# The long-convolution filter moved into the steps of expert layer 0

## The chip, the core and the metric

The kernel runs on one core of one Trainium2 chip. The metric is the device time of one execution in microseconds. Before the change it is 1826.23 us, the median of three runs (1824.58 to 1829.15).

## What is computed

Two blocks of a diffusion backbone over 256 tokens of width 1024, plus 256 context tokens in the first block, all in float32. Block 0 mixes tokens with a bidirectional RWKV, block 1 with an order-2 Hyena operator; after each comes a mixture of experts with 32 experts, top-2. Cut to what matters here:

```python
def _hyena_filters(L, f_w1, f_b1, f_freq, f_wi, f_bi, f_w3):       # needs weights only, no tokens
    hdn = jnp.sin(f_freq * (z @ f_w1 + f_b1))                      # 33 -> 64
    for n in range(2):
        hdn = jnp.sin(f_freq * (hdn @ f_wi[n] + f_bi[n]))          # 64 -> 64
    h = (hdn @ f_w3).reshape(L, 2, 2, D) * jnp.exp(-t * deltas)    # 64 -> 2 orders x 2 signs x 1024
    kern = jnp.concatenate([h[:, :, 0], 0, flip(h[1:, :, 1])])
    return kern / jnp.sum(jnp.abs(kern), 0)
def _fft_conv(u, kern, skip):                                      # twice in _hyena_seq
    return irfft(rfft(u) * rfft(kern))[:L] + u * skip
def expert_block(args):                                            # for each of 32 experts
    return (silu(xb @ w_gate[e]) * (xb @ w_up[e])) @ w_down[e]     # 1024x512, 1024x512, 512x1024
```

## The kernel before

The program is a row of blocks with a barrier between them: RWKV, `expert_layer` for layer 0, `hyena_layer` (two blocks, `hyena_inputs` and `hyena_convolutions`), `expert_layer` for layer 1, and the final norm. SBUF is one arena in which every stage lays out its own tiles by column.

**Expert layer.** All 32 experts' weights are streamed through SBUF once in each layer: 96 units of 2 MB (128 partitions with one row of 16 KB each), in the order gate, up, down of each step. Ten steps: steps 0 to 3 are wide (two experts, six units), steps 4 to 9 narrow (four experts, twelve units, numbers 24 to 95). The units go round a ring of `SLOTS_OF` = 10 slots of the arena. `expert_units` writes the order by hand: for each unit its slot and the unit that held the slot before. SP, in program order, waits (`unit_done`) until that earlier unit's product has ended and issues the load (line 1770; the last step's down units are cut into quarters, line 1768). Semaphore `block_in` tells TensorE of the landing. The first `FIRST_UNITS` = 6 units are issued in the stage before. A small batch of loads that the next stage needs (`gate_b`, `hyena.load_small`, the 1154 KB `hy_const`) stands ahead of unit 88 in the same queue.

TensorE's order in step i: gate product (line 1935, bank G), up product (line 1935, bank U), gather of step i+1's tokens (line 1922, banks X0 and X1), turning the hidden rows (lines 1963 and 1965), scatter of step i-1 (line 1983), down product (line 1945, into X0 and X1). A product of a narrow step needs all four units of its kind and frees all four at its end. ScalarE applies the Silu to G, turns tokens and copies the down result out of X0 and X1 (`copy_rows`, lines 2073 and 2074, semaphore `y_ready`). VectorE multiplies gate by up (`hidden_rows`, line 2149) and, in steps 1 to 3, works through twelve possible extra expert slots (`take_extras`, then `count_extras`, line 2295).

**`hyena_inputs`.** 24 input products `in_block` (line 2579), each of 16 instructions of 256 columns, with the filter's pieces placed between them by hand (`taps_after`, `spectrum_after`): three sine layers (`argument`, `sine`), the taps times a window (`taps`, `windowed`, lines 2712 to 2716), forward transforms (`spectrum`, line 2551; `combine`), sums of magnitudes (`absolute`, `magnitudes`, `turn_magnitudes`). **`hyena_convolutions`** transforms the values, multiplies by `khat` and transforms back, then the output product. SP starts layer 1's expert units here: two at the start, then four after `y_done` reaches 8; units 6 to 9 follow at the start of layer 1.

## Time and profile before

| | us |
|---|---|
| median of three runs | 1826.23 |
| the profiled execution | 1815.37 |
| its span in the trace | 1813.2 |
| layer 0 stream, first issue to last chunk used | 619 to 1106 |
| `hyena_inputs` | 1119 to 1247 |
| `hyena_convolutions` | 1247 to 1335 |
| layer 1 | 1335 to 1803 |

All rows come from the one profiled execution; times in them are microseconds from the start of its span. The page divides the span into 40 slices. A line of the timeline merges consecutive instructions of a kind; the bracket gives the engine's idle time before it and what ended it. "PE" is TensorE, "DVE" VectorE, "ACT" ScalarE, "SPq" and "ACTq" the queues on which SP and ScalarE issue transfers. For a transfer the timeline's duration is the time in which the issuing queue was held, not the transfer's. TensorE's granted clock is given as a share of its full 2.4 GHz.

### The profile page before, as it was taken

How to read it: one execution, taken by the hardware profiler on the slowest of the kernel's cores; microseconds unless marked ns; L12 is line 12 of the kernel's file. 1: busy time of each engine (PE TensorE's matmuls, PEld its weight loads, DVE VectorE, ACT ScalarE, POOL GpSimd, SP SyncE). 2: the span in 40 equal slices, each digit the busy share in tenths (PEclk: the TensorE clock that was granted, in tenths of full speed). 3: DMA queues.
4: the chain of work that ended last, by engine and by line, in shares of the span. 5: the costliest groups of instructions: out<-in, count | busy, mean ns of one | idle time of the engine just before them, and what ended most of it. 6: DMA issues, size and time to landing. Idle time of an engine off the chain costs nothing. (4 is left out here: it accounts for less than half of the span.)

```text
span 1813.2 us, 35471 instructions
## 1 busy us (share of the span) xinstructions
PE 1412.5 (78%) x14647; PEld 781.5 (43%) x14647; DVE 758.6 (42%) x1952; ACT 448.8 (25%) x857; POOL 57.9 (3%) x53
## 2 busy tenths in 40 slices
PE   5879999999986989966455737998899985557545
PEld 2446766676665443422122203776544341222111
DVE  5767787778764365400000001766757510000001
ACT  3244565456543031110000002213131110000001
POOL 0001100110010000000000001000000000000001
PEclk8989999999998999987787769999999997887788
DMA  9023334424445599999999997224279999999995
GB/s 333 1 63 100 105 115 133 125 89 130 118 138 191 183 427 427 426 427 427 428 428 428 427 384 274 93 93 185 77 322 393 425 428 427 427 427 428 427 426 224
DMA packets 108946, 504.55 MB, mean 278 GB/s; under 512 B 16224, under 2 KB 61040, under 8 KB 83952
## 3 DMA queue, kind: packets, MB, share of 16 engines
q1 hardware_dynamic: 107520, 501.93, 69.9%
q8 instruction: 118, 1.93, 0.4%
q10 hardware_dynamic: 1264, 0.33, 0.1%
q14 instruction: 44, 0.36, 0.1%
HBM read 501.13 MB, written 1.09 MB: 277 GB/s over the span
## 5 line engine op out<-in xcount | busy, mean ns | idle before, releaser
L1935 PE MATMUL banks<-arena 128*32 128x512 f32 (+1 forms) x2048 | 326.1, 689 | 241.7 <-DMA arena<-in_moe_w_gate 121.6
L1935 PEld LDWEIGHTS banks<-arena 128*32 128x32 f32 (+1 forms) x2048 | 97.7, 131 | 467.6 <-issue 464.0
L2149 DVE TENSOR_TENSOR arena<-banks,arena 128x512 f32<-128x512 f32 x20 | 13.8, 692 | 631.3 <-PE banks L1935 631.0
L1945 PE MATMUL banks<-arena 128*32 128x512 f32 (+1 forms) x1024 | 147.0, 615 | 32.0 <-DMA arena<-in_moe_w_down 29.9
L788 PE MATMUL banks<-arena 128*128 128x512 f32 (+1 forms) x384 | 158.7, 551 | 0.0
L2063 ACT ACTIVATE arena<-banks,arena 128x128 f32<-128x128 f32 x80 | 30.1, 457 | 303.2 <-PE banks L1922 303.2
L1945 PEld LDWEIGHTS banks<-arena 128*32 128x32 f32 (+1 forms) x1024 | 46.2, 119 | 129.6 <-issue 121.7
L788 PEld LDWEIGHTS banks<-arena 128*128 128x128 f32 x384 | 70.3, 196 | 52.5 <-issue 44.3
L2579 PE MATMUL banks<-arena 128*128 128x256 f32 x384 | 87.4, 386 | 0.0
L2579 PEld LDWEIGHTS banks<-arena 128*128 128x128 f32 x384 | 73.5, 193 | 16.7 <-issue 6.6
L1922 PEld LDWEIGHTS banks<-arena 128*128 128x128 f32 x640 | 73.0, 192 | 16.7 <-issue 14.9
L1922 PE MATMUL banks<-arena 128*128 128x128 f32 x640 | 76.8, 278 | 0.1
L2054 ACT ACTIVATE arena<-banks 128x512 f32<-128x512 f32 x20 | 11.9, 597 | 260.8 <-PE banks L1935 260.8
L1983 PE MATMUL banks<-arena 128*128 128x512 f32 x160 | 72.2, 594 | 2.4 <-ACT arena L2074 2.4
L2073 ACT ACTIVATE arena<-banks 128x512 f32<-128x512 f32 x20 | 11.9, 597 | 211.7 <-PE banks L1945 211.7
L253 PE MATMUL banks<-arena 128*32 128x96 f32 (+1 forms) x1536 | 46.5, 260 | 12.4 <-DMA arena<-in_ada_w 11.1
L2061 DVE TENSOR_SCALAR arena<-banks,arena 128x128 f32<-128x128 f32 x80 | 27.3, 403 | 53.5 <-PE banks L1922 53.5
L253 PEld LDWEIGHTS banks<-arena 128*32 128x32 f32 x1536 | 35.0, 110 | 21.5 <-issue 17.7
L1983 PEld LDWEIGHTS banks<-arena 128*128 128x128 f32 x160 | 28.8, 190 | 32.9 <-issue 28.7
L1214 ACT ACTIVATE arena<-x_res,const 128x256 f32<-128x256 f32 x64 | 42.2, 733 | 1.4 <-DVEq L1469 0.6
L2349 POOL TENSOR_TENSOR x_res<-x_res,arena 128x512 f32<-128x512 f32 x8 | 9.9, 1265 | 971.7 <-DVEq L2323 971.7
L2287 DVE TENSOR_TENSOR arena<-arena 128x128 f32<-128x128 f32 x120 | 35.1, 292 | 9.6 <-issue 0.7
(412 smaller groups left out, 2293.0 us busy)
## 6 DMA issues: line engine op xcount, KB each, us to landing
arena<-in_moe_w_gate SPq DMA_DIRECT2D x64, 2048.0 KB, 25.2
arena<-in_moe_w_up SPq DMA_DIRECT2D x64, 2048.0 KB, 27.0
arena<-in_moe_w_down SPq DMA_DIRECT2D x56, 2048.0 KB, 25.2
arena<-in_ada_w SPq DMA_DIRECT2D x128, 192.0 KB, 3.0
arena<-in_ada_w SPq DMA_DIRECT2D x64, 256.0 KB, 3.6
arena<-in_moe_w_down SPq DMA_DIRECT2D x32, 512.0 KB, 17.1
arena<-in_rw_wrkv SPq DMA_DIRECT2D x24, 512.0 KB, 5.2
arena<-in_hy_w_in SPq DMA_DIRECT2D x6, 2048.0 KB, 8.6
```

The source lines that it names most:

```text
L253: mm = pe.matmul(bank[g * 32:(g + 1) * 32, 0:n], self.cond[:, half * self.HALF + t], self.w[t][:, g * n:(g + 1) * n], start=(t == 0), stop ...
L788: mm = pe.matmul(s.psum[OPEN.bank(n, name)][:, 0:width], wkv[k][:, t], x[:, t], start=(t == 0), stop=(t == KT - 1))
L1214: act.activation(to, v, ACT.Identity, scale=flag(d))
L1922: mm = pe.matmul((X0, X1)[k // 4][:, k % 4 * P:(k % 4 + 1) * P], hx[:, t, k * P:(k + 1) * P], sel[:, t], start=(t == 0), stop=(t == TT - 1))
L1935: mm = pe.matmul(bank[j * rows:(j + 1) * rows, :], xT[:, t, j * rows:(j + 1) * rows], w[:, t], start=(t == 0), stop=(t == KT - 1), tile_po ...
L1945: mm = pe.matmul(bank[j * rows:(j + 1) * rows, :], hT[:, t, j * rows:(j + 1) * rows], w[:, k, half * 512:(half + 1) * 512], start=(t == 0) ...
L1983: pe.matmul(OUT[k][:, :], selwT[par][:, k // 2], y[:, k % 2 * 512:(k % 2 + 1) * 512], start=start, stop=stop).then_inc(scat_done, 1)
L2061: op = eng.tensor_scalar(xT[:, k], src, sc[:, k:k + 1], sh[:, k:k + 1], ALU.mult, ALU.add)
L2063: op = eng.activation(xT[:, k], src, ACT.Identity, bias=sh[:, k:k + 1], scale=sc[:, k:k + 1])
L2149: dve.tensor_tensor(h, U[:, :], h, ALU.mult).then_inc(h_ready, 1)
L2287: dve.tensor_tensor(prod, pick, src, ALU.mult)
L2579: mm = pe.matmul(s.psum[n % 2][:, 0:L], win_ring[k][:, t, q * P:(q + 1) * P], hT[:, t], start=(t == 0), stop=(t == KT - 1))
```

## The change

The filter leaves `hyena_inputs`. A new class `HyenaFilter` computes it in eleven pieces inside expert layer 0 (`FILTER_WORK`): two in each of steps 3 to 7, ahead of the gate product and ahead of the up product, and one in step 8. Pieces 0 to 2 are the sine layers. Pieces 3 to 10 each take a quarter of the 1024 channels of one order: taps, window, forward transform, sum and difference into `khat`, magnitudes, reciprocal. They run in banks X0 and X1, so TensorE waits in front of each for `y_ready`, and the gather waits for the pieces' reads.

The filter's small weights and half of `hy_const` are now issued by SP ahead of unit 18 (`load_constants`). The output weights of the filter and the decay rates come in four quarters, issued on ScalarE's queue (`load_quarter`): quarter 0 at the start of step 4, and quarter q+1 when ScalarE has done the second piece of quarter q, since one buffer serves all. Each quarter is two transfers of 64 partitions x 2 rows and two of 128 rows, rows of 1 KB.

The spectra, constants and scratch take over ring slots of layer 0: slots 8 and 9 leave the ring at unit 10, slot 7 at unit 24 and slot 3 at unit 84, so that ten slots become eight, seven and six. In layer 1 only slot 3 leaves, at unit 84 (before, slot 8 left at 79). With the new tables a unit's slot was held before it, in layer 0, by: unit 18 by 10; 29 by 22; 31 by 24; units 32 to 83 by the unit seven before; 90 by 84 and 94 by 88. `hyena_inputs` keeps the 24 input products. Layer 1's unit 0 is issued at its end, unit 1 after the second `imag_ready`, units 2 and 3 after `y_done` reaches 8, and from unit 4 on at the start of layer 1.

```diff
-FIRST_UNITS = 6
-TAIL_UNITS = 79
...
+LAST = 3
+RETIRED = ({WORK: 10, TAIL: 10, 7: 24, LAST: 84}, {LAST: 84})
+FIRST_UNITS = (6, 4)
...
-                if slot == TAIL and n >= TAIL_UNITS:
-                    slot = WORK
+                while n >= retired.get(slot, n + 1):
+                    slot = (slot + 1) % SLOTS_OF
...
-UNITS, LAST_IN = expert_units()
+UNITS, LAST_IN = zip(*(expert_units(r) for r in RETIRED))
+N_UNITS = len(UNITS[0])
...
-            for n in range(SLOTS_OF, len(UNITS)):
-                step = UNITS[n][0]
...
+            now, early, late = None, fil is not None, True
+            for n in range(SLOTS_OF, N_UNITS):
+                step, used = units[n][0], units[n][6]
                 if step >= FIXED // 2 and step != now:
                     now = step
                     first, count = (2 * step - FIXED, 2) if step < WIDE_STEPS else (HOT + 4 * (step - WIDE_STEPS), 4)
                     if step == FIXED // 2:
                         sp.wait_ge(moved_ready, 1)
                     of = [sp.value_load(moved_i[0:1, k:k + 1], min_val=0, max_val=EXPERTS - 1) for k in range(first, first + count)]
-                sp.wait_ge(unit_done, UNITS[n][6] + 1)
-                if UNITS[n][6] == LAST_IN[TAIL] + 1:
+                sp.wait_ge(unit_done, used + 1)
+                if early and used > last_in[TAIL] and used > last_in[WORK]:
+                    early = False
+                    fil.load_constants(sp, ins)
+                if late and used > last_in[LAST]:
+                    late = False
                     sp.dma_start(gate_b, experts.mod_row(mods, 5).partition_broadcast(P)).then_inc(gate_in, 16)
                     if hyena is not None:
                         hyena.load_small(sp, ins, mods)
                 experts.load_unit(sp, ins, n, fixed(step) if step < FIXED // 2 else of)
             if hyena is not None:
                 for b in range(hyena.SLOTS):
-                    sp.wait_ge(unit_done, LAST_IN[b] + 1)
+                    sp.wait_ge(unit_done, last_in[b] + 1)
                     hyena.load_ring(sp, ins, b)
...
+            if fil is not None and isinstance(i, int):
+                fil.banks_read(pe, i - 1)
...
                 tokens_ready(pe, i)
+                if fil is not None and (i, 0) in FILTER_WORK:
+                    pe.wait_ge(y_ready, i)
+                    fil.multiply(pe, FILTER_WORK.index((i, 0)))
                 hidden_product(pe, i, "gate", G)
+                if fil is not None and (i, 1) in FILTER_WORK:
+                    pe.wait_ge(y_ready, i)
+                    fil.multiply(pe, FILTER_WORK.index((i, 1)))
                 hidden_product(pe, i, "up", U)
                 if i + 1 < N_STEPS:
...
             for i in range(N_STEPS):
+                if fil is not None and i == EXTRA // 4 + 1:
+                    act.wait_ge(extra_ready, 1)
+                    fil.load_quarter(act, ins, 0)
+                if fil is not None and (i, 0) in FILTER_WORK:
+                    fil.activate(act, ins, FILTER_WORK.index((i, 0)))
                 silu_gate(act, i)
+                if fil is not None and (i, 1) in FILTER_WORK:
+                    fil.activate(act, ins, FILTER_WORK.index((i, 1)))
                 if i + 1 < N_STEPS:
                     turned_rows(act, range(4, KT), i + 1).then_inc(xT_act, 1)
...
+                for gap in range(2):
+                    if fil is not None and (i, gap) in FILTER_WORK:
+                        fil.combine(dve, FILTER_WORK.index((i, gap)))
                 hidden_rows(dve, i)
...
+    def load_constants(self, sp, ins):
+        hy = self.hy
+        for n, v in enumerate((ins["hy_f_freq"][0], ins["hy_f_b1"][0], ins["hy_f_bi"][0, 0], ins["hy_f_bi"][0, 1])):
+            sp.dma_start(hy.fv[0:FH, n:n + 1], v.unsqueeze(1)).then_inc(hy.w_in, 16)
+            if n in (0, 3):
+                sp.dma_start(hy.fv[FH:P, n:n + 1], v.unsqueeze(1)).then_inc(hy.w_in, 16)
+        sp.dma_start(hy.w1[0:EMB, :], ins["hy_f_w1"][0]).then_inc(hy.w_in, 16)
+        sp.dma_start(hy.wi[0:FH], ins["hy_f_wi"][0].rearrange("n i o -> i n o")).then_inc(hy.w_in, 16)
+        sp.dma_start(hy.hc, ins["hy_const"][:, 0:HY_EARLY]).then_inc(hy.hc_in, 16)
+
+    def load_quarter(self, act, ins, q):
+        c = slice(q * 256, (q + 1) * 256)
+        for od in range(2):
+            rows = ins["hy_f_w3"][0, :, od * 2 * D:(od + 1) * 2 * D].rearrange("r (a n) -> r a n", a=2)
+            act.dma_start(self.hy.f_w3[od * FH:(od + 1) * FH], rows[:, :, c]).then_inc(self.f3_in, 16)
+        for i in range(TT):
+            act.dma_start(self.hy.window[:, i], ins["hy_deltas"][c].partition_broadcast(P)).then_inc(self.delta_in, 16)
+
...
+            pe.wait_ge(self.read, k)
+        if k == 0:
+            pe.wait_ge(hy.hc_in, 16)
+            pe.wait_ge(hy.w_in, 128)
+            pe.matmul(self.banks[0][0:FH, 0:L], hy.w1[0:EMB, :], hy.hc[0:EMB, 0:L], start=True, stop=True).then_inc(self.f_done, 1)
+        elif k < SINES:
+            pe.wait_ge(self.hd_ready, k)
+            for od in range(k):
+                mm = pe.matmul(self.banks[0][od * FH:(od + 1) * FH, 0:L], hy.wi[0:FH, k - 1], hy.hd[0:FH, :], start=True, stop=True)
+            mm.then_inc(self.f_done, 1)
+        else:
+            q, od = self.unit(k)
+            u, at = k - SINES, slice(od * FH, (od + 1) * FH)
+            pe.wait_ge(self.hd_ready, SINES)
+            pe.wait_ge(self.f3_in, 32 * (q + 1))
+            for i in range(TT):
+                mm = pe.matmul(self.banks[i][:, :], hy.hd[at, i * P:(i + 1) * P], hy.f_w3[at].rearrange("p a n -> p (a n)"), start=True, stop=True)
+            mm.then_inc(self.taps_done, 1)
+            pe.wait_ge(self.taps_ready, u + 1)
+            for part in range(2):
+                for i in range(TT):
+                    mm = pe.matmul(self.banks[part][:, i * 256:(i + 1) * 256], hy.fwd[part][:, i, 0:P], hy.both[:, part, i], start=True, stop=True)
+            mm.then_inc(self.spec_done, 1)
+            pe.wait_ge(self.abs_ready, u + 1)
+            for m in range(2):
+                for i in range(TT):
+                    mm = pe.matmul(self.banks[0][:, 2 * m:2 * m + 2], hy.both[:, 0, i, m * P:(m + 1) * P], ones[:, 0:2], start=(i == 0), stop=(i == TT - 1))
+            mm.then_inc(self.abs_done, 1)
+
+    def activate(self, act, ins, k):
+        hy = self.hy
+        if k < SINES:
+            act.wait_ge(self.arg_done, k + 1)
+            rows_of = slice(0, P if k == 2 else FH)
+            act.activation(hy.hd[rows_of, :], hy.arg[rows_of, :], ACT.Sin).then_inc(self.hd_ready, 1)
+        else:
+            q, od = self.unit(k)
+            u = k - SINES
+            if od == 0:
+                act.wait_ge(self.delta_in, 32 * (q + 1))
+                for i in range(TT):
+                    act.activation(hy.window[:, i], hy.window[:, i], ACT.Exp, scale=hy.minus_t[:, i:i + 1]).then_inc(self.win_ready, 1)
+            act.wait_ge(self.spec_done, u + 1)
+            act.activation(hy.even, self.pair[:, :, 0:256], ACT.Copy).then_inc(self.even_ready, 1)
+            act.activation(hy.both, hy.both, ACT.Abs).then_inc(self.mag_ready, 1)
+            if od and q < 3:
+                self.load_quarter(act, ins, q + 1)
...
+            return
+        q, od = self.unit(k)
+        u, c = k - SINES, slice(q * 256, (q + 1) * 256)
+        h0, h1 = hy.even, hy.turns2
+        dve.wait_ge(self.win_ready, TT * (q + 1))
+        dve.wait_ge(self.taps_done, u + 1)
+        dve.tensor_tensor(h0, self.pair[:, :, 0:256], hy.window, ALU.mult)
+        for i in range(TT):
+            dve.scalar_tensor_tensor(h1[:, i], self.pair[:, i, 256:512], hy.keep[:, i:i + 1], hy.window[:, i], ALU.mult, ALU.mult)
+        dve.drain()
+        dve.tensor_tensor(hy.both[:, 0], h0, h1, ALU.add)
+        dve.tensor_tensor(hy.both[:, 1], h0, h1, ALU.subtract)
+        dve.drain()
+        dve.sem_inc(self.taps_ready, 1)
+        dve.wait_ge(self.even_ready, u + 1)
+        for part in range(2):
+            a, b = hy.even[:, part], self.pair[:, part, 256:512]
+            dve.tensor_tensor(hy.khat[od][part][:, 0, c], a, b, ALU.add)
+            first, second = ((a, b), (b, a))[part]
+            dve.tensor_tensor(hy.khat[od][part][:, 1, c], first, second, ALU.subtract)
+        dve.wait_ge(self.mag_ready, u + 1)
+        dve.tensor_tensor(hy.both[:, 0], hy.both[:, 0], hy.both[:, 1], ALU.max)
+        dve.drain()
+        dve.sem_inc(self.abs_ready, 1)
+        dve.wait_ge(self.abs_done, u + 1)
+        m = od * CH + 2 * q
+        dve.reciprocal(hy.norm[:, m:m + 2], self.banks[0][:, 0:4:2]).then_inc(self.read, 1)
...
         def _(sp):
-            for i in range(TT):
-                sp.dma_start(window[:, i], ins["hy_deltas"].partition_broadcast(P)).then_inc(win_in, 16)
-            sp.wait_ge(chv_done, 1)
-            for od in range(2):
-                sp.dma_start(f_w3[od * FH:(od + 1) * FH, :], ins["hy_f_w3"][0, :, od * 2 * D:(od + 1) * 2 * D]).then_inc(f3_in, 16)
+            sp.dma_start(inverse, ins["hy_const"][:, HY_EARLY:].rearrange("p (n i f) -> p n i f", n=2, i=2)).then_inc(inv_in, 16)
             for b in range(SLOTS, BLK // 4):
                 sp.wait_ge(in_done, 4 * (b - SLOTS) + 4)
                 hy.load_ring(sp, ins, b)
+            experts.load_unit(sp, ins, 0, [0, 1])
...
             pe.wait_ge(hT_ready, KT)
-            layer1()
             for n in range(BLK):
                 in_block(n)
-                if n < 2:
-                    inner_layer(n)
-                if n in taps_after:
-                    taps(taps_after.index(n))
-                if n in spectrum_after:
-                    spectrum(spectrum_after.index(n))
-                if n == BLK - 2:
-                    magnitudes()
-            turn_magnitudes()
-            pe.wait_ge(spec_ready, 4)
...
             sp.dma_start(b_out, ins["hy_b_out"][0].partition_broadcast(P)).then_inc(row_in, 16)
-            for n in range(2):
-                experts.load_unit(sp, ins, n, [0, 1])
+            sp.wait_ge(imag_ready, 2)
+            experts.load_unit(sp, ins, 1, [0, 1])
             sp.wait_ge(y_done, 8)
             experts.load_rows(sp, ins, mods)
-            for n in range(2, FIRST_UNITS):
+            for n in range(2, FIRST_UNITS[1]):
                 experts.load_unit(sp, ins, n, [0, 1])
...
+                if od == 0:
+                    pe.wait_ge(inv_in, 16)
...
-        expert_layer(s, experts[0], ins, mods, hyena)
+        expert_layer(s, experts[0], ins, mods, hyena, HyenaFilter(s, hyena))
```

## Rows read from the trace of the kernel before

**Rows 1.** The page, section 2: DMA rate in 40 slices of 45.3 us.

```profile
GB/s 333 1 63 100 105 115 133 125 89 130 118 138 191 183 427 427 426 427 427 428 428 428 427 384 274 93 93 185 77 322 393 425 428 427 427 427 428 427 426 224
```

**Rows 2.** Stretch of one narrow step: busy us, granted clock, DMA share, GB/s.

```profile
850.00:908.57 58.57, 32.52 (x243) 12.99 (x239) 2.81 (x7) 3.95 (x9) 0.00 (x0) 0.83 1.01 428
```

**Rows 3.** Timeline, layer 0, steps 5 and 6; last row from step 8.

```profile
860.45 7.07 PE L1945 MATMUL banks<-arena 128*32 128x512 f32 x64 [2.51 <-DMA arena<-in_moe_w_down]
867.58 0.60 ACT L2073 ACTIVATE arena<-banks 128x512 f32<-128x512 f32 x1 [11.47 <-PE banks L1945]
880.03 8.55 PE L1935 MATMUL banks<-arena 128*32 128x512 f32 x64 [12.51 <-DMA arena<-in_moe_w_gate]
899.61 9.00 PE L1935 MATMUL banks<-arena 128*32 128x512 f32 x64 [11.03 <-DMA arena<-in_moe_w_up]
908.54 3.84 PE L1922 MATMUL banks<-arena 128*128 128x128 f32 x32
...
1017.11 9.97 PE L1935 MATMUL banks<-arena 128*32 128x512 f32 x64 [10.05 <-DMA arena<-in_moe_w_up]
```

**Rows 4.** The page, section 3: DMA packets by size.

```profile
DMA packets 108946, 504.55 MB, mean 278 GB/s; under 512 B 16224, under 2 KB 61040, under 8 KB 83952
```

**Rows 5.** The tile in_rw_mix, loaded by ACT's queue at the start.

```profile
L393 ACTq DMA_DIRECT2D arena<-in_rw_mix x1: 418/418/418, 4.6 to 4.6; - x1
DMA to landing us min/median/max: 18.1/18.1/18.1
```

**Rows 6.** The tile in_ada_b, four loads on ACT's queue.

```profile
DMA to landing us min/median/max: 20.9/21.9/23.1
```

**Rows 7.** The tile in_moe_w_up, loads of 2 MB.

```profile
DMA to landing us min/median/max: 8.1/27.0/40.1
```

**Rows 8.** Timeline, layer 0, steps 1 and 2.

```profile
713.14 0.81 SPq L1770 DMA_DIRECT2D arena<-in_moe_w_up  x2
...
749.19 0.17 DVE L2295 CAST arena<-arena 128x13 int32<-128x13 f32 x1
```

**Rows 9.** Timeline, layer 0, step 9: two small loads, the last chunk's product.

```profile
1030.07 7.12 SPq L2419 DMA_DIRECT2D arena<-in_hy_f_freq  x1
...
1056.41 0.42 SPq L2428 DMA_DIRECT2D arena<-in_hy_const  x1
...
1105.61 1.92 PE L1945 MATMUL banks<-arena 128*32 128x512 f32 x16 [2.37 <-DMA arena<-in_moe_w_down]
```

**Rows 10.** Two stretches of step 9 in layer 0.

```profile
1056.00:1060.00 4.00, 3.62 (x20) 1.13 (x24) 0.00 (x0) 0.00 (x0) 0.00 (x0) 0.50 0.90 233
1072.00:1080.00 8.00, 0.00 (x0) 0.00 (x0) 0.00 (x0) 0.00 (x0) 0.00 (x0) 0.50 1.01 432
```

**Rows 11.** Timeline, TensorE in the first hyena block.

```profile
1131.02 5.41 PE L2579 MATMUL banks<-arena 128*128 128x256 f32 x16
...
1190.22 3.60 PE L2551 MATMUL banks<-arena 128*128 128x512 f32 x8
1221.22 17.43 PE L2579 MATMUL banks<-arena 128*128 128x256 f32 x80
1247.49 7.17 PE L2808 MATMUL banks<-arena 128*128 128x512 f32 x16 [1.15 <-PEq L2500]
```

**Rows 12.** Timeline, ScalarE and VectorE in the same block.

```profile
1146.94 1.28 ACT L2657 ACT_TABLE_LOAD   x1
1148.23 2.19 ACT L2657 ACTIVATE arena<-arena 128x1024 f32<-128x1024 f32 x2
...
1163.18 0.69 DVE L2712 TENSOR_TENSOR arena<-banks,arena 128x512 f32<-128x512 f32 x1
```

**Rows 13.** Timeline, SP, start of expert layer 1.

```profile
1334.96 0.80 SPq L1770 DMA_DIRECT2D arena<-in_moe_w_gate  x2
...
1361.31 0.80 SPq L1770 DMA_DIRECT2D arena<-in_moe_w_down  x2
```

**Rows 14.** Stretch of time in layer 1 just before its eleventh unit.

```profile
1358.00:1362.00 4.00, 4.00 (x22) 1.62 (x20) 3.61 (x10) 0.60 (x1) 0.00 (x0) 1.00 0.00 0
```

More of the change, by code:

```diff
@@ L738, in _ @@
             experts.load_rows(sp, ins, mods)
-            for n in range(FIRST_UNITS):
+            for n in range(FIRST_UNITS[0]):
                 experts.load_unit(sp, ins, n, [0, 1])
@@ L1761, in load_unit @@
     def load_unit(self, sp, ins, n, of):
-        _, kind, part, cut, slot, _, _ = UNITS[n]
+        _, kind, part, cut, slot, _, _ = self.units[n]
         if cut:
@@ L1772, in weights @@
     def weights(self, n):
-        _, kind, _, cut, slot, _, _ = UNITS[n]
+        _, kind, _, cut, slot, _, _ = self.units[n]
         width = D if kind == "down" else HIDDEN
@@ L1800, in expert_layer @@
     assert s.at <= 2 * experts.large
+    s.at = experts.last
+    acc = s.take(TT, D)
+    rows_b = s.take(D)
     s.at = experts.routing
@@ L2387 @@
 HY_BLK = 3 * CH
+HY_EARLY = L + 2 * TT + 2 * 2 * 256
 class HyenaTensors:
@@ L2396, in __init__ @@
         self.ring = s.arena[:, experts.large * 2:experts.large * 3].rearrange("p (b t n) -> p b t n", b=2, t=KT)
-        s.at = experts.large * 5 + TT * D + 2 * 2 * D
-        self.constants = s.at
-        self.hc = s.take(HY_CONST.shape[1])
+        s.at = experts.unit
+        first = s.take(2, 2, D)
+        s.at = experts.work
+        second = s.take(2, D)
+        self.even, self.both = s.take(2, 256), s.take(2, TT, 256)
+        self.arg, self.turns = s.take(L), s.take(L)
+        self.turns2 = s.arena[:, s.at - 2 * L:s.at].rearrange("p (i n) -> p i n", i=TT)
+        assert s.at <= experts.work + experts.unit
+        s.at = experts.tail
+        self.khat = [[first[:, 0], first[:, 1]], [s.take(2, D), second]]
+        self.hc = s.take(HY_EARLY)
+        self.minus_t, self.keep = self.hc[:, L:L + TT], self.hc[:, L + TT:L + 2 * TT]
+        o = L + 2 * TT
+        self.fwd = [self.hc[:, o + n * 512:o + (n + 1) * 512].rearrange("p (i f) -> p i f", i=2) for n in range(2)]
         self.w1, self.wi = s.take(FH), s.take(2, FH)
         self.fv = s.take(4)
+        self.hd = s.take(L)
         self.sc, self.sh, self.ng = s.take(KT), s.take(KT), s.take(KT)
         self.skip, self.norm = s.take(16), s.take(16)
-        s.at = self.constants - 2 * P
         self.rows, self.rows2 = s.take(P), s.take(P)
+        s.at = experts.routing
+        self.f_w3, self.window = s.take(2, 256), s.take(TT, 256)
+        assert s.at <= experts.small
         sem = lambda n: s.nc.alloc_semaphore(name="hy_" + n)
@@ L2436, in hyena_layer @@
     win_ring = [hy.ring[:, k] for k in range(SLOTS)]
-    hc = hy.hc
-    zT = hc[:, 0:L]
-    minus_t, keep = hc[:, L:L + TT], hc[:, L + TT:L + 2 * TT]
-    o = L + 2 * TT
-    fwd = [hc[:, o + n * 512:o + (n + 1) * 512].rearrange("p (i f) -> p i f", i=2) for n in range(2)]
-    inv = [hc[:, o + (2 + n) * 512:o + (3 + n) * 512].rearrange("p (i f) -> p i f", i=2) for n in range(2)]
-    w1, wi, fv = hy.w1, hy.wi, hy.fv
+    fwd, khat = hy.fwd, hy.khat
     sc, sh, ng, skip, norm = hy.sc, hy.sh, hy.ng, hy.skip, hy.norm
     rows, rows2 = hy.rows, hy.rows2
-    s.at = 0
-    window = s.take(TT, D)
-    hT = s.take(KT, L)
+    s.at = experts.large
+    tmp = s.take(2, D)
+    s.at = experts.work + 2 * D
+    inverse = s.take(2, 2, 256)
+    inv = [inverse[:, n] for n in range(2)]
+    s.at = experts.work + experts.unit
     up = [s.take(L + 2) for _ in range(2)]
-    hd = s.take(L)
-    arg, turns = s.take(L), s.take(L)
     chv = s.take(P)
@@ L2526, in taps @@
-            def taps(g):
-                i, half = tap_groups[g]
-                if g == 0:
-                    pe.wait_ge(hd_ready, 3)
-                    pe.wait_ge(f3_in, 32)
-                else:
-                    pe.wait_ge(taps_ready, 2 * g)
-                for sign in range(2):
-                    c = sign * D + half * 512
-                    for od in range(2):
-                        at = slice(od * FH, (od + 1) * FH)
-                        mm = pe.matmul(s.psum[TAPS[od * 2 + sign]][:, :], hd[at, i * P:(i + 1) * P], f_w3[at, c:c + 512],
-                                       start=True, stop=True)
-                mm.then_inc(taps_done, 1)
@@ L2554, in magnitudes @@
-            def magnitudes():
-                pe.wait_ge(abs_ready, 1)
-                for i in range(TT):
-                    for g in range(4):
-                        od, half = divmod(g, 2)
-                        mm = pe.matmul(s.psum[7][g * 32:(g + 1) * 32, :], s.c("ones")[:, 0:32], hsum[:, od, i, half * 512:(half + 1) * 512],
-                                       start=(i == 0), stop=(i == TT - 1), tile_position=(0, g * 32))
-                        if i == TT - 1:
-                            mm.then_inc(abs_done, 1)
```

267 lines of the change are left out of this document (88 added, 179 removed).

## Prediction

> **What bounds the kernel now.** I read the DMA rate by slice first: 14 or so slices at 427 GB/s are the two expert layers, and the Hyena block between them moves 77 to 322 [rows 1]. A narrow step lasts 58.6 us with the DMA share at 1.01 and TensorE 32.5 us busy [rows 2], and its products wait for weights [rows 3]. Four units take 880.03 - 860.45 = 19.58 us, so a unit 4.9 [rows 3]. The expert layers are thus set by the stream of units; `hyena_inputs` is set by TensorE, whose products follow each other (five in 17.43 us, 3.47 each) [rows 11]. The idea of the change is to put filter work into TensorE's idle 26 us per step. The questions are what leaves the Hyena block, whether the stream of layer 0 stays full, and when layer 1's stream starts.
>
> **Hyena block: -28 us.** Without the filter the 24 products run back to back: the first takes 5.4 [rows 11], 23 more 3.47 each, 85 us from 1130.5 (half a us early, the first sine product being gone), so they end at 1215.7. The four transposes and value copies at the end stay; from the last product before (1221.22 + 17.43, then 1.9 of magnitudes and 3.6) to 1247.49 is 3.5 us. The next block starts at 1219.2 instead of 1247.49 [rows 11]: 28.3 us. VectorE's 1.6 us and ScalarE's 0.5 us per product stay under 3.47. `w_in` blocks land in 8 to 9 us and are used in 14, so they stay hidden; if that cover were gone, it would be a rival (below). The convolutions keep their operations.
>
> **Layer 1: +3.5 us.** Four units are ahead instead of six. Before, units 6 to 9 are issued from 1334.96, have landed by 1358, and DMA stands still until unit 10 is issued at 1361.31, when the first gate product frees its slot [rows 13, 14]. After, six units (4 to 9) follow the block's start: 1.6 + 6 x 4.9 = 31 us, against 27.5 us before to the start of unit 10 (1362.5). The stream is late by 3.5 us and from then on full. Slot 3 leaving at unit 84 instead of slot 8 at 79 costs nothing: nine slots stay either way.
>
> **Layer 0, the constants: +7 us, then +3.** Counting back 34 units from 880.03 [rows 3], unit 17 lands at 713.6. Unit 18 now waits for unit 10, freed at 713.14 [rows 8] (before, for unit 8), and nine small loads stand ahead of it. A small issue holds the queue 0.42 us when it isn't blocked [rows 9], so unit 18 is issued at 717.3. An issue into an idle queue lands after 8.1 us [rows 7]: 725.4 instead of 718.5, +7. In the trace the same loads held SP from 1030.07 to 1056.41 [rows 9] behind a full queue; here it is nearly empty, and I take the short end (long end: +20 more). Step 3's sines: VectorE is busy with extras until 749.19 [rows 8], so the first sine is ready at 752.5, the up product starts 2.2 us late after y_ready's 1.2, and the down product ends near 775 instead of 770.3. Unit 29 (slot of 22) is issued then and lands at 783.2 instead of 780: +3.
>
> **Layer 0, one piece.** TensorE's taps are four instructions of 512 columns at 0.45 (3.60 for 8), the transforms eight of 256 at 0.22 [rows 11]. VectorE has some four passes of 0.69 [rows 12], ScalarE 0.6 for 512 elements [rows 3] and 1.1 for 1024 [rows 12]. An even piece (ahead of the gate product): taps 1.9, window 3.0, transforms 2.0, copy and four sums 2.3, maximum 0.7, magnitudes 1.0, semaphores: 11.2 us. From the down product's end plus 1.3 for the copies [rows 3] to the gate units' landing there are 11.2 us, and from the gate product's end to the up units' landing 11.0 [rows 3]. An odd piece has Silu, a set load of 1.28 and two exponentials of 0.45 first [rows 12], 12.3 us in all. So TensorE's time would just fit. Seven slots bear a little lateness: three units are in flight behind four held ones, they land 14.7 us after the group, and a new issue must come 3.2 us before that (8.1 - 4.9): 11.4 us after landing. Products take 8.6 to 10.0 now [rows 3].
>
> **Layer 0, the quarters: +44 us, the term that decides.** Odd pieces in steps 4 to 7 need a quarter that ScalarE's queue loads while SP's queue is full. The nearest rows: `in_rw_mix`, 24 KB in 768 rows of 32 bytes, landed 18.1 us after its issue [rows 5], and four loads of 64 KB after 20.9 to 23.1 [rows 6], all beside SP's 8 KB rows of `in_ada_w`. A unit's row is one packet of 16 KB (108,946 less 83,952 = 24,994 packets of 8 KB or more; 184 uncut units have 23,552 rows) [rows 4]. A quarter has 512 rows, 32 per engine: 32 x 0.612 + 3.2 = 23 us. If instead ScalarE's queue were served when SP's backlog is gone, it would be about 20. I take 23.
>
> Quarter 0 is issued at 776.3, lands at 799.3. Then exponentials 0.9, window 3.1, transforms 2.1, sums 3.0, magnitudes 1.0: 10 us; TensorE has idled 13 us by then, its granted clock is 0.50 after such a wait [rows 10], and products after one take 8.6 to 10.0 instead of 7.07 [rows 3]: +2.5 (bounds 0 and 4). The up product ends at 799.3 + 10 + 2.5 + 7.1 = 818.9, only then is unit 35 issued, and it lands at 827.2 instead of 801.5: +25.7, of which 10 are counted above. Behind the waiting ScalarE stand the token copies and `copy_hidden`, behind TensorE the gather; they only follow. Quarters 1 to 3 are issued when the even piece's magnitudes are done, 8.5 (up end to down start [rows 3], 908.54 less gather) + 7.1 + 1.3 + 9.0 = 25.9 us after the up product. The period becomes 23 + 10 + 2.5 + 7.1 + 25.9 = 68.5 us instead of 58.7: three times 9.8 is 29. In sum +55 by the down product of step 7. The quarters' own bytes (4.9 us) run in the gaps.
>
> **Layer 0, the end: -3 us.** Step 9 took 49.2 us from its gate units (1056.4) to the last chunk (1105.61) [rows 9], with a thin queue on the way (233 GB/s) [rows 10]; eight units are 39.2. Six slots cost 2.3 before the up units and 2.7 before the last down units, small loads 1.5: 46 us. The `w_in` blocks 0 and 1 are issued 40 us later than now, but land within 12 us of the last chunk and are needed 25 us after it: hidden.
>
> **Sum.** Layer 0 +52 (7 + 3 + 16 + 29 - 3), Hyena -28.3, layer 1 +3.5: +27 us. The profiled execution has 1815.4 us (span 1813.2), which becomes 1842.6. The median is 1826.2, so 1853.
>
> **Rivals.** *Prompt quarters* (faster): the quarters land within 10.7 us of issue, before the window is wanted. For it: 0.5 MB is 1.2 us of data, 4.4 us with the 3.2; a 16 KB row may be served in shares; the rows at the start are of 32 bytes, which may be slow by themselves. Against it: rows 5 and 6 as counted. Layer 0 then costs 7 + 3 + 1 + 4.9 of bytes - 3 = 13, in all -12 us: 1814. It decides below L = 15 us, where the period's excess ends. The Trainium skill, "DMA: Bandwidth & Descriptors", section "Anatomy of one DMA", gives a transfer about 2.0 us plus its bytes at 436 GB/s, for the software path; 0.5 MB would be 3.2 us, an estimate by that page that no row here shows on a busy queue, and it would give this rival's time.
>
> *Thin ring*: quarters prompt, but seven slots starve by themselves, since products that end 10 us after landing [rows 3] and a piece that runs 1 to 2 us over pass the 11.4: 1 us at each of 15 groups, +15, in all +3: 1829.
>
> *Hyena not TensorE-bound*: the products wait for `w_in` or the convolution chain, and the block gives back little. Rows against it: TensorE without a gap in 17.43 us [rows 11]. It would add up to 28: 1881.
>
> **Chances.** Forecast (quarters late) 0.57, prompt 0.29, thin ring 0.10, Hyena 0.04. The forecast's own range: L of 20 and no cold penalty gives +4.7 (period 63), L of 24 and 4 us gives +34 to +36: 1831 to 1862. The range reaches to the prompt case: 1811 to 1864. About 0.3% (5.5 us) is what a measurement of this kernel can tell from no change: faster 0.29, same 0.12 (thin ring and the forecast's low end), slower 0.59.
>
> **What would show it.** Right: in steps 4 to 7 TensorE or ScalarE waits for `in_hy_deltas` on ScalarE's queue, landing near 23 us; narrow steps of 68 us in 5 to 7 and of 59 in step 8; DMA gaps of some 10 us before each last down unit; `hyena_inputs` of 100 us without gaps in its products; layer 1's stream full 31 us after its start. Wrong: quarters landing in under 15 us, narrow steps of 59 us; or gaps before unit 18 of 20 us, as behind a blocked queue.

## The result, and the profile after

The changed kernel takes 1879.6 us in the median (1871.8 to 1885.6) against 1825.4 (1816.6 to 1829.2) for the kernel before on the same chip: a ratio of 1.0291, 95% interval 1.0256 to 1.0326, or 54 us more. The forecast was 27 more. The profiled execution has 1885.25 us (span 1883.4). It issued the first unit of layer 0 14.0 us later than the profiled execution of before (633.09 against 619.07), in code that the change doesn't touch; so I count every stage from its own start.

| stretch | before, us | after, us | difference | forecast |
|---|---|---|---|---|
| unit 0 issued to last down chunk's product, layer 0 | 486.5 | 569.2 | +82.6 | +52 |
| first product of the Hyena block's input stage to its convolutions | 128.2 | 97.8 | -30.3 | -28.3 |
| convolutions up to layer 1's first issues | 87.5 | 88.4 | +0.9 | 0 |
| layer 1 | 456.3 | 459.2 | +2.8 | +3.5 |

The sum is +56, against +54 between the medians. The miss lies in layer 0 alone. The rate by slice, which answers to [rows 1], shows it at a glance: in layer 0 the steady 427 of before has become a comb of high and low slices, in layer 1 it is whole.

```profile
GB/s 321 1 61 111 109 109 109 135 108 109 126 142 157 254 427 330 411 263 414 307 314 404 300 421 389 262 92 157 132 174 427 426 427 428 427 427 427 428 427 224
```

Step 5, which has a quarter's load, and under it step 8, which has none to wait for (windows; columns as in [rows 2]): step 5 takes 75.0 us against 58.6, TensorE busy for 50.4 instead of 32.5 at a mean granted clock of 0.70 instead of 0.83, and the DMA share down from 1.01 to 0.83.

```profile
839.30:914.30 75.00, 50.40 (x282) 22.88 (x278) 13.07 (x31) 10.51 (x17) 0.00 (x0) 0.70 0.83 343
...
1063.90:1121.66 57.76, 40.10 (x262) 17.27 (x259) 7.94 (x19) 6.78 (x12) 0.00 (x0) 0.82 0.98 410
```

The timeline of step 5, which answers to [rows 3]. The quarter is asked for at 865.79, straight behind the copy of the even piece. The taps wait for the weights of the filter until 883.00, the exponentials for the decay rates until 893.41, 27.6 us after the first issue. All else is in line behind that: window, transforms at half speed (3.78 us for eight, 1.9 at full clock), magnitudes, and the up product (8.78, where the forecast had 7.1; before the change such a product took 9.00 [rows 3], but hidden behind the stream), on whose end the next four units of the stream wait.

```profile
865.79 0.61 ACTq L2513 DMA_DIRECT2D arena<-in_hy_f_w  x1
...
867.10 1.09 ACTq L2515 DMA_DIRECT2D arena<-in_hy_deltas  x2
...
870.31 9.37 PE L1948 MATMUL banks<-arena 128*32 128x512 f32 x64
...
883.00 3.75 PE L2536 MATMUL banks<-arena 64*128 64x512 f32 x4 [3.33 <-DMA arena<-in_hy_f_w]
...
893.41 0.91 ACT L2561 ACTIVATE arena<-arena 128x256 f32<-128x256 f32 x2 [11.76 <-DMA arena<-in_hy_deltas]
...
897.28 3.78 PE L2541 MATMUL banks<-arena 128*128 128x256 f32 x8 [10.54 <-DVEq L2597]
...
905.63 8.78 PE L1948 MATMUL banks<-arena 128*32 128x512 f32 x64
```

The waits by engine (instruction, what it waited for: us in all, times, longest) show the same for all four quarters, and the loads' landing answers to [rows 5, 6]:

```profile
ACT arena L2561 <- DMA arena<-in_hy_deltas: 53.6, 4, 17.6
...
PE banks L2536 <- DMA arena<-in_hy_f_w: 19.9, 4, 9.1
```

```profile
DMA to landing us min/median/max: 16.1/23.3/26.1
```

How the loads get through is in the trace's records of transfers. Between the first row of quarter 1 and the next gap in the stream (869.5 to 881) SP's queue (q1) and ScalarE's (q10) moved (packets, MB, share of the 16 DMA engines):

```profile
q1 hardware_dynamic: 284, 4.13, 93.5%
q10 hardware_dynamic: 279, 0.26, 6.8%
```

Without the packets of 4 bytes these are 252 rows of 16 KB and 254 rows of 1 KB: one for one. Where one engine's records can be followed from end to start, 385 of 464 successions (870 to 881) go from one queue to the other. The first row moved at 869.6, 3.8 us after the first issue; the last ended at 892.3, 1.1 us before the exponentials.

The Hyena block did what was forecast. Against [rows 11], its 24 products are one unbroken run of 84.83 us (timeline, TensorE):

```profile
1202.27 3.31 PE L1958 MATMUL banks<-arena 128*32 128x512 f32 x16 [3.92 <-DMA arena<-in_moe_w_down]
...
1225.93 84.83 PE L2688 MATMUL banks<-arena 128*128 128x256 f32 x384 [2.34 <-ACT arena L2730]
...
1313.66 6.74 PE L2809 MATMUL banks<-arena 128*128 128x512 f32 x15 [1.15 <-PEq L2668]
```

At unit 18 the DMA engines stood still, longer than forecast. Windows (last column GB/s), and the issues of SP beside them, which answer to [rows 8]:

```profile
724.00:728.00 4.00, 4.00 (x22) 1.41 (x20) 3.19 (x12) 0.00 (x0) 0.00 (x0) 1.00 0.10 41
728.00:732.00 4.00, 4.00 (x22) 1.31 (x20) 3.19 (x12) 1.09 (x2) 0.00 (x0) 1.00 0.04 0
732.00:736.00 4.00, 4.00 (x20) 1.29 (x18) 2.38 (x9) 0.60 (x1) 0.00 (x0) 1.00 0.46 109
```

```profile
728.09 0.53 SPq L2502 DMA_DIRECT2D arena<-in_hy_f_freq  x1
...
733.95 0.88 SPq L1774 DMA_DIRECT2D arena<-in_moe_w_gate  x2
```

In layer 1, the counterpart of [rows 13, 14]: the eleventh unit is issued 26.0 us after the block's start (1402.05), into a queue that is still full (DMA share 1.01 from 1424 to 1428, where before the change it had been 0.00).

```profile
1428.05 0.80 SPq L1774 DMA_DIRECT2D arena<-in_moe_w_down  x2
```

Layer 0's 82.6 us by step, from the end of one up product to that of the next (before, after): step 3 28.6 and 33.3; step 4 36.2 and 64.3; steps 5, 6, 7 58.4, 58.6, 58.4 and 75.0, 74.1, 75.5; step 8 60.1 and 57.7; from there to the last chunk 78.5 and 80.5. The rest, 0.9, came ahead of step 3.

### The profile page after: what moved, and what is told of

Read it like the earlier page. It is cut to its first block and busy times, and to the rows that moved or that the text cites. A ratio compares the mean times of both kernels' runs of the same rounds, so it can differ in the third digit from the quotient of the medians.

```text
span 1883.4 us, 35721 instructions
## 1 busy us (share of the span) xinstructions
PE 1466.6 (78%) x14723; PEld 818.2 (43%) x14723; DVE 762.8 (40%) x1996; ACT 456.8 (24%) x871; POOL 57.7 (3%) x53
## 5 line engine op out<-in xcount | busy, mean ns | idle before, releaser
L2175 DVE TENSOR_TENSOR arena<-banks,arena 128x512 f32<-128x512 f32 x20 | 13.8, 692 | 452.2 <-PE banks L1948 451.9
L788 PEld LDWEIGHTS banks<-arena 128*128 128x128 f32 x384 | 70.1, 196 | 52.4 <-issue 44.2
L2688 PE MATMUL banks<-arena 128*128 128x256 f32 x384 | 84.8, 385 | 2.3 <-ACT arena L2730 2.3
L1935 PEld LDWEIGHTS banks<-arena 128*128 128x128 f32 x640 | 73.0, 192 | 16.7 <-issue 14.9
L2688 PEld LDWEIGHTS banks<-arena 128*128 128x128 f32 x384 | 74.0, 193 | 12.9 <-ACT arena L2730 2.5
L2541 PE MATMUL banks<-arena 128*128 128x256 f32 x64 | 29.7, 643 | 54.3 <-DVEq L2597 54.3
L2591 DVE TENSOR_TENSOR arena<-banks,arena 128x512 f32<-128x512 f32 x8 | 5.5, 692 | 149.2 <-ACT arena L2561 95.8
L2541 PEld LDWEIGHTS banks<-arena 128*128 128x128 f32 x64 | 20.1, 330 | 69.0 <-DVEq L2597 64.7
L1994 PEld LDWEIGHTS banks<-arena 128*128 128x128 f32 x160 | 28.8, 190 | 33.7 <-issue 28.7
```

The source lines that it names most:

```text
L788: mm = pe.matmul(s.psum[OPEN.bank(n, name)][:, 0:width], wkv[k][:, t], x[:, t], start=(t == 0), stop=(t == KT - 1))
L1935: mm = pe.matmul((X0, X1)[k // 4][:, k % 4 * P:(k % 4 + 1) * P], hx[:, t, k * P:(k + 1) * P], sel[:, t], start=(t == 0), stop=(t == TT - 1))
L1994: pe.matmul(OUT[k][:, :], selwT[par][:, k // 2], y[:, k % 2 * 512:(k % 2 + 1) * 512], start=start, stop=stop).then_inc(scat_done, 1)
L2175: dve.tensor_tensor(h, U[:, :], h, ALU.mult).then_inc(h_ready, 1)
L2541: mm = pe.matmul(self.banks[part][:, i * 256:(i + 1) * 256], hy.fwd[part][:, i, 0:P], hy.both[:, part, i], start=True, stop=True)
L2688: mm = pe.matmul(s.psum[n % 2][:, 0:L], win_ring[k][:, t, q * P:(q + 1) * P], hT[:, t], start=(t == 0), stop=(t == KT - 1))
```

## The experiments

Each ratio is to the kernel before on the same chip. A difference in us from the changed kernel is one of medians, partly taken on different chips, where the kernel before had 1824.6 to 1827.4 us; it is uncertain by some 3 us for that. The theory after the result: the quarters' loads take turns with the units' rows of 16 KB, each row of a quarter waiting for one of a unit, and this landing, counted four times, is what makes layer 0 long.

**The dose.** `one_decay` loads the decay rates once per quarter and forms both exponentials from that copy; `half_rows` splits each load of decay rates in two of half the width.

`one_decay`:

```diff
-        for i in range(TT):
-            act.dma_start(self.hy.window[:, i], ins["hy_deltas"][c].partition_broadcast(P)).then_inc(self.delta_in, 16)
+        act.dma_start(self.hy.window[:, 0], ins["hy_deltas"][c].partition_broadcast(P)).then_inc(self.delta_in, 16)
...
-                for i in range(TT):
-                    act.activation(hy.window[:, i], hy.window[:, i], ACT.Exp, ...
+                for i in (1, 0):
+                    act.activation(hy.window[:, i], hy.window[:, 0], ACT.Exp, ...
```

`half_rows`:

```diff
-            act.dma_start(self.hy.window[:, i], ins["hy_deltas"][c].partition_broadcast(P)).then_inc(self.delta_in, 16)
+            for h in range(2):
+                act.dma_start(self.hy.window[:, i, h * 128:(h + 1) * 128],
+                              ins["hy_deltas"][q * 256 + h * 128:q * 256 + (h + 1) * 128].partition_broadcast(P)).then_inc(self.delta_in, 16)
```

> The changed kernel, but each quarter's decay rates are loaded once and not twice, so ScalarE's queue has 24 rows for each DMA engine in place of 32. Theory (each row of this queue waits for one row of SP's queue, 0.65 us): the second exponential's data is there 8 x 0.65 = 5.2 us sooner, from first issue to exponential 22.4 us in place of 27.6, and the narrow steps with a load go from 75 to about 70 us: 16 to 21 us less in all, about 1861. Rival (the loads are served only once the backlog of SP's queue is gone): the exponential starts where it did, less one issue of 0.5 us: 0 to 2 us less in all.

> The changed kernel, but each load of decay rates is split into two of 512 B per partition, so each DMA engine has 48 rows of ScalarE's queue per quarter in place of 32, with the same bytes. Theory (turns are taken row for row, whatever a row's size): 16 rows x 0.65 = 10.4 us, and some 1 us for two more issues, later for each quarter: narrow steps with a load of about 86 us in place of 75, and 40 to 46 us more in all, about 1922. Rival (the landing goes by bytes, or by the backlog of SP's queue): 1 us more per quarter, about 1884.

`one_decay`: 1861.8 us, ratio 1.0183 (1.0155 to 1.0211), 17.8 less than the changed kernel. `half_rows`: 1921.0, ratio 1.0519 (1.0489 to 1.0549), 41.4 more. Both came out as the theory had it. The exponentials of one quarter (timeline, ScalarE; the quarter's first issue, then its exponentials), first in `one_decay`, then in `half_rows`:

```profile
855.80 0.61 ACTq L2513 DMA_DIRECT2D arena<-in_hy_f_w  x1
...
878.41 0.91 ACT L2560 ACTIVATE arena<-arena 128x256 f32<-128x256 f32 x2 [6.55 <-DMA arena<-in_hy_deltas]
```

```profile
871.91 0.61 ACTq L2513 DMA_DIRECT2D arena<-in_hy_f_w  x1
...
909.57 0.91 ACT L2563 ACTIVATE arena<-arena 128x256 f32<-128x256 f32 x2 [21.60 <-DMA arena<-in_hy_deltas]
```

From first issue to exponential, mean of quarters 1 to 3: 22.2 us with 24 rows per DMA engine, 27.5 with 32, 37.3 with 48. The slope is 15.1 / 24 = 0.63 us per row, at one and the same number of bytes between 32 and 48; the intercept 7 us. A unit's row of 16 KB takes 0.61 us at the full rate. So bytes don't count, and a row of 512 B waits as long as one of 1 KB. By the dose alone it could be turns of whole transfers just as well, since each transfer has 8 rows per engine in all three kernels (3, 4 and 6 transfers). The records decide for rows: in the changed kernel 252 to 254 within 11.5 us, as above, and in `half_rows` (961 to 992) 737 rows of 16 KB to 753 of the quarter's. The steps 5 to 7 followed about one to one: 68.7, 67.7, 68.6 us in `one_decay`, 84.9, 82.6, 84.8 in `half_rows`.

**The same loads on the other queue.** `sp_queue` issues the same rows from SP, in line with the units.

```diff
             for n in range(SLOTS_OF, N_UNITS):
...
+                if quarter_at and used >= quarter_at[0]:
+                    q = 4 - len(quarter_at)
+                    quarter_at = quarter_at[1:]
+                    sp.wait_ge(*((fil.mag_ready, 2 * q) if q else (extra_ready, 1)))
+                    fil.load_quarter(sp, ins, q)
                 sp.wait_ge(unit_done, used + 1)
```

Here `quarter_at` holds the first down unit of step 3 and the first gate units of steps 5, 6 and 7; the calls on ScalarE are gone.

> The changed kernel, with the same four quarter loads at the same places of the work, but issued on SP's queue, in line with the units and ahead of the four units that the gate product behind the even piece sets free. Same rows of 1 KB, same bytes, same DMA engines. Theory (a row of 1 KB is cheap by itself, and dear on ScalarE's queue only because it takes turns with rows of 16 KB): a quarter waits for at most the three units in flight, 14.7 us, less what has landed since their issue, so it lands 5 to 18 us after its issue in place of 23 to 28, narrow steps of 60 to 67 us in place of 75, about 1842. Rival (rows of 1 KB to all partitions cost some 0.64 us each whatever stands beside them): landing stays above 22 us, 1875 or above.

1846.1 us, ratio 1.0099 (1.0082 to 1.0116), 33.6 less than the changed kernel. Steps 5 to 7 took 71.0, 68.5 and 70.8 us, longer than the 60 to 67 expected, and the time is 4 us over the forecast of 1842. The landing of the decay rates:

```profile
DMA to landing us min/median/max: 15.1/16.3/18.0
```

A row of 1 KB is thus not dear by itself. SP had issued three up units some 11 us ahead of quarters 1 to 3; in line behind what is left of them the decay rates land in 15 to 18 us, of which ScalarE waits for only 5 to 7 (three times, 17.9 us in all).

**No wait for a quarter at all.** `quarters_ahead` keeps the load on ScalarE's queue and asks early: for quarter 0 in step 3, for 1 at that step's end, for 2 at the end of step 4, and for 3 once quarter 0 is worked off. Quarters 1 and 2 go into the columns of the spectra that quarter 3 fills last.

```diff
+        ahead = [[k[part][:, :, 3 * 256:D] for part in range(2)] for k in self.khat]
+        self.of_quarter = [(self.f_w3, self.window), ahead[0], ahead[1], (self.f_w3, self.window)]
...
-            if od and q < 3:
-                self.load_quarter(act, ins, q + 1)
+            if k == SINES + 1:
+                self.load_quarter(act, ins, 3)
...
+                if fil is not None and i == EXTRA // 4:
+                    act.wait_ge(extra_ready, 1)
+                    fil.load_quarter(act, ins, 0)
...
+                if fil is not None and i == EXTRA // 4:
+                    fil.load_quarter(act, ins, 1)
+                if fil is not None and i == EXTRA // 4 + 1:
+                    fil.load_quarter(act, ins, 2)
```

> The changed kernel, but quarters 0, 1 and 2 are asked for in steps 3 and 4, the second and third into the columns of the spectra that quarter 3 fills last, and quarter 3 once quarter 0 is worked off. No piece should then wait for its data. Theory (the landing is what the steps wait for, the pieces' own work is about hidden): narrow steps of 59 to 63 us in place of 75, 35 to 50 us less in all, about 1835. Rival (the pieces' own chain on TensorE and VectorE makes the steps long even when their data is there): steps of 68 us or more, 1855 or above.

1828.0 us, ratio 1.0005 (0.9983 to 1.0028): 51.7 less than the changed kernel and level with the kernel before. No instruction waits for `in_hy_f_w` or `in_hy_deltas` any more. Steps 5 to 7 have 62.2, 67.6 and 61.6 us where 75.0, 74.1 and 75.5 were, and step 4 47.5 instead of 64.3. So the waits for the landing were worth 52 us. In this trace layer 0 is still 32 us longer than before (518.7 us against 486.5), about what the Hyena block gives back.

**What is left: the clock.** `ahead_warm` adds, to `quarters_ahead`, products of a constant into the free bank U while TensorE waits in a piece.

```diff
             mm.then_inc(self.taps_done, 1)
+            self.s.keep_warm(pe, self.s.psum[1], 3)
             pe.wait_ge(self.taps_ready, u + 1)
...
             mm.then_inc(self.spec_done, 1)
+            self.s.keep_warm(pe, self.s.psum[1], 3)
             pe.wait_ge(self.abs_ready, u + 1)
```

> The kernel with the quarters ahead, and in each of the eight pieces three products of a constant into the free bank of the up product while TensorE waits for the windowed taps, and three more while it waits for the magnitudes. Theory (what is left of the filter's cost in layer 0 is TensorE at its low clock: transforms 3.78 us, magnitudes 1.86 us, gate and up products 8.5 to 9.4 us, where 1.9, 0.9 and 7.1 us are to be had): each piece and the product behind it give back some 4 us, the narrow steps with pieces fall from 62.2, 67.6 and 61.6 us to 58 to 60 us, where the weights' transfer takes over, 12 to 18 us less in all, about 1813, which is below the kernel before. Rival (the clock isn't to be had back so, or the added products lengthen the chain by as much): 1825 or above.

1819.7 us, ratio 0.9971 (0.9956 to 0.9986): faster than the kernel before by 0.3%. It is 8.2 us less than `quarters_ahead` by the medians, which are from two chips, 6 by the two ratios, and 8.9 in layer 0 of the two traces. The granted clock in steps 5 to 7 rose from 0.81, 0.77, 0.81 to 0.92, 0.97, 0.92. The same piece and product in both kernels (timeline, TensorE), first without and then with the added products:

```profile
970.34 3.78 PE L2549 MATMUL banks<-arena 128*128 128x256 f32 x8 [3.03 <-DVEq L2606]
...
978.01 8.57 PE L1948 MATMUL banks<-arena 128*32 128x512 f32 x64
```

```profile
968.28 1.89 PE L2550 MATMUL banks<-arena 128*128 128x256 f32 x8
970.01 2.74 PE L94 MATMUL banks<-const 128*128 128x512 f32 x6
...
972.94 1.05 PE L2556 MATMUL banks<-const,arena 128*128 128x2 f32 x8 [0.19 <-DVEq L2618]
973.92 7.07 PE L1948 MATMUL banks<-arena 128*32 128x512 f32 x64
```

Transforms 3.78 to 1.89 us, and the product behind them 8.57 to 7.07. The size missed, 6 to 8 us instead of 12 to 18: the narrow steps took 63.9, 58.1 and 62.3 us where 58 to 60 were expected, with waits for weights in them and the DMA share at 1.00 to 1.01, so not all that TensorE gave back could be had. Of the three only step 6 became shorter.

**The ring and the constants.** `ring_alone` is the kernel before with the ring tables of the change in layer 0 and nothing else; `constants_ahead` and `ahead_warm_lean` issue the constants once unit 17 is issued.

`ring_alone`:

```diff
-TAIL_UNITS = 79
+LAST = 3
+RETIRED = ({9: 10, 8: 10, 7: 24, LAST: 84}, {8: 79})
...
-                if slot == TAIL and n >= TAIL_UNITS:
-                    slot = WORK
+                while n >= retired.get(slot, n + 1):
+                    slot = (slot + 1) % SLOTS_OF
```

`constants_ahead`:

```diff
+                if early and n == 18:
+                    early = False
+                    sp.wait_ge(unit_done, 10)
+                    fil.load_constants(sp, ins)
```

> The kernel before, with the ring tables of the change in layer 0 alone: slots 8, 9 and 7 are retired at units 10 and 24 and the slot of the last rows at unit 84, and nothing of the filter is moved. Theory (the quarters' loads and the pieces make the 82.6 us, the thin ring nearly nothing): within 4 us of the kernel before, about 1829. Rival (a ring of seven slots leaves too little in flight for rows of 16 KB): 15 us or more over the kernel before, 1840 or above, with narrow steps over 62 us in place of 58.7.

1839.8 us, ratio 1.0077 (1.0038 to 1.0117): 12 to 14 us over before. The theory (within 4 us) missed, and the rival's narrow steps of over 62 us didn't come either. Steps 5 to 8 took 59.2, 58.4, 60.1 and 58.4 us (58.4, 58.6, 58.4 and 60.1 before), so the ring doesn't starve in its run. In the trace the cost stands in two places: the up product of step 4 ends 6.7 us late, behind a hole in the stream at unit 18 (windows),

```profile
711.90:715.90 4.00, 4.00 (x22) 1.29 (x18) 3.19 (x12) 0.00 (x0) 0.00 (x0) 1.00 0.69 295
715.90:719.90 4.00, 4.00 (x21) 1.29 (x18) 3.19 (x12) 1.08 (x2) 0.00 (x0) 1.00 0.30 61
```

and 8.2 us come after step 8. `ring_small_late` differs from it in one number, the unit ahead of which the 20 small loads stand (88 as in the kernel before, where `ring_alone` has 84).

> The kernel before with the thin ring of layer 0, as before, but its 20 small loads stand ahead of unit 88, where the kernel before has them, and not ahead of unit 84. Theory (of the 15.7 us that the thin ring cost in layer 0, 7.2 are the gap at unit 18 and 8.3 are at the end, where the small loads hold up SP's queue while the ring runs empty): the gap at unit 18 stays, the end costs 2 to 4 us in place of 8.3, about 1834. Rival (the end is dear since seven slots, then six, are too few for the last two steps): 1839, as with the small loads ahead of unit 84.

1834.8 us, ratio 1.0044 (1.0028 to 1.0061). The end now costs 4.8 us and no longer 8.2, at step 4 it is 5.8 late. So part of the end was the small loads on a queue that runs empty, and the other part goes with the retired slots, by one trace of each kernel: their times overlap (1834.1 to 1849.4 and 1834.0 to 1836.3).

> The changed kernel, but the nine constants are issued on SP's queue before the wait of unit 18, while the ring is still full. Theory (their issues of 5.3 us stand between a drained ring and unit 18, so the DMA engines are idle that much longer): 5 to 9 us less, about 1873. Rival (unit 18 waits for its slot anyway and the stages behind take the gap in): under 2 us less.

1880.8 us, ratio 1.0279 (1.024 to 1.0319): nothing gained, although the hole shrank from 9.6 us of idle DMA engines to 1.6 (windows around the issue of unit 18 at 722.79):

```profile
720.00:724.00 4.00, 4.00 (x22) 1.29 (x18) 3.19 (x12) 1.09 (x2) 0.00 (x0) 1.00 0.78 202
724.00:728.00 4.00, 4.00 (x21) 1.29 (x19) 3.19 (x12) 0.00 (x0) 0.00 (x0) 1.00 0.82 324
```

The up product of step 4 ends 206.2 us after unit 0's issue with the hole shrunk and 206.3 with it. It waits for quarter 0, which ScalarE asks for when step 3 is over (156.1 and 156.9 us after unit 0's issue), and in neither kernel does TensorE wait for a weight in step 3.

> The same with the decay rates loaded once per quarter and the constants ahead of unit 18's wait. Theory (no piece waits for its data any more, so fewer rows give nothing; the gap of the DMA engines at unit 18 is that of the thin ring): within 3 us of the kernel with the quarters ahead and warm waits. Rival (the rows still cost the weights' transfer their turns, and the gap is the issues'): 5 us or more less.

1818.9 us, ratio 0.9972 (0.9955 to 0.9989), 0.9 under `ahead_warm`: no difference that can be told.

## Why the prediction went wrong, step by step

- **What bounds it, Hyena block, layer 1: right.** -30.3 against -28.3, +2.8 against +3.5; the products' run was forecast at 85 us and takes 84.8. The rival that the block isn't bound by TensorE falls.
- **The mechanism that decides: right.** ScalarE's rows take turns with SP's, one for one: 0.63 us per row by dose, 0.612 forecast. The rival of prompt quarters falls: the decay rates landed 16.1 to 26.1 us after their issue, and `sp_queue` shows that it is the company of the other queue that makes these rows dear. The Trainium skill, "DMA: Bandwidth & Descriptors", section "Anatomy of one DMA", gives 3.2 us for a quarter, an estimate by that page's formula for the software path; the trace of a second queue beside a loaded one doesn't agree with it (16.1 to 26.1 us). The Trainium skill, "DMA: Bandwidth & Descriptors", section "Queues, rings and completion order", has each DMA engine go round the queues that have work and drain a whole packet, typically some 9 to 17 descriptors, before it switches. The trace agrees with the turns, but here a turn is one row, by its records: 254 rows of 1 KB against 252 of 16 KB.
- **The term that was mis-sized: the landing L = 23 us.** It was 32 x 0.612 + 3.2, where the 3.2 had been read off one unit of 2 MB on an idle queue. Measured from the first of the quarter's four issues to the exponentials it is 27.5 (28.5 for quarter 0). The slope was right within 1 us (32 x 0.63 = 20.2 against 19.6); what stands beside it is 7 us and not 3.2. The records of quarters 1 to 3 divide it: 3.9 us until the first row moves, 22.4 from the first row to the last, which is 2.3 over the slope's 20.2, and 1.1 until the exponentials. The four issues (865.79 to 868.19) were over before the first row moved, so they add nothing of their own. A row of 16 KB took 0.68 us in the mean while the two queues took turns (869.5 to 881), 0.61 alone, and the sum had 0.612 for it. Of the 4.5 us that the term was short, about 2.8 are thus the rows (22.4 where it had 19.6) and 1.8 the wait before the first and behind the last (5.0 where it had 3.2). My upper bound of 24 for L was thus too low as well. The term counts four times: 5.5 + 3 x 4.5 = 19 us.
- **The cold clock: named, but not carried through.** The forecast had +2.5 for the piece (its bounds 0 and 4) and took 7.1 for the up product. The piece came out as forecast (12.2 us from exponential to product), but the product itself runs 8.7, 8.8, 9.7 and 9.3 us in steps 4 to 7: 1.6 to 2.6 more, 8 us in all. [rows 3] had shown 8.6 to 10.0 for a product after idle time, which I quoted and then used only in part.
- **The constants: a real hole, counted as if it were on the path.** The hole was 9.6 us, not 7, and closing it gave nothing, since the next thing on the path, quarter 0's issue, hangs on TensorE's step 3 and not on the stream. That issue was forecast at 776.3 and came at 790.02 - 14.0 = 776.0; the 7 and the 3 did no harm to the sum, because the forecast had itself taken them off what quarter 0 costs.
- **The end: -3 forecast, about 0 measured** (-2.4 in step 8, +2.0 after it), 3 us. In `ring_small_late`, with the small loads where they were before, the thin ring makes the stretch behind step 8 4.8 us longer, where I had it 3 shorter. The changed kernel has fewer small loads there; what each of the two does in it stays open.
- **Thin ring: wrong as a rival by itself, not nothing.** It doesn't act at each of 15 groups but at the two places where slots leave, 12 us in all by `ring_alone`. In the changed kernel shrinking the hole at the first place gave nothing back (`constants_ahead`), since step 4 waits for quarter 0.

The landing's 19, the products' 8 and the end's 3, less 1 for the pieces (12.2 us where 12.5 was forecast, four times), are 29 of the 31 us that layer 0 has over the forecast. The period shows it too: 25.9 + 27.5 + 12.1 + 9.3 = 74.8 us against 25.9 + 23 + 12.5 + 7.1 = 68.5.

The mechanism was right and the price of its main term too low. By the forecast's own terms the upper end (L of 24, 4 us for the cold clock) comes to +37, about 1863, and not to +34 to +36; even so it lies some 16 us under the result.

## What to carry to other kernels

A small load on a second DMA queue beside a stream of large rows is priced by its rows, not its bytes (rows of 1 KB and 512 B here): rows per DMA engine times the time of the stream's row, and to that some 7 us here; make it few rows, ask for it a step ahead, or put it in line on the stream's own queue. When one latency sits in a loop, its whole chain, from the first issue to the first use, belongs in the term, since an error of 4.5 us is paid each time round. A hole in the stream costs only if the stream is what the next step waits for.

## What the runs showed that I had not expected

- With the decay rates in twice as many rows of half the size, the same bytes were ready 10 us later (37.3 against 27.5 us).
- 9.6 us of idle DMA engines in a kernel whose layers are bound by DMA could be closed without any gain (1880.8 against 1879.6 us).
- Filling TensorE's waits was worth 6 to 8 us: added products that compute nothing brought the transforms from 3.78 to 1.89 us and the product behind them from 8.6 to 7.07.
